# Split fp32r products for a trunk's dense projections, and a turned gather in the expert passes

## The reference

```python
z = x @ w_in + b_in                      # 1024 -> u_a 512, u_b 512, z_ga 1024, z_gb 1024
out_a = pool_mixer(u_a, ...)             # windowed means of 2, 4, 8, 16 rows, then w_pool per group
y, h  = ssm_mixer(u_b, ...)              # S5: diagonal complex recurrence, 32 groups x 64 states
out_b = gelu(y) * sigmoid(gelu(y) @ w_glu + b_glu)
merged = sigmoid(z_ga) * (out_a @ w_proj_a) + sigmoid(z_gb) * (out_b @ w_proj_b)
x = layer_norm(ALPHA * x + merged @ w_out)
# layer 0: dense SwiGLU 1024 -> 2816 -> 1024; layer 1: top 2 of 8 experts, 1024 -> 3584 -> 1024
x = layer_norm(ALPHA * x + ffn(x))
```

## Time and profile before

| | |
|---|---|
| median of 3 runs | 1784.83 us (1780.98 to 1785.2) |
| profiled execution, its own time | 1787.87 us |
| its span | 1786.0 us |
| mean granted TensorE clock | 0.976 of full |
| TensorE busy | 1730.0 us, 97% |
| VectorE busy | 1175.3 us, 66% |
| ScalarE busy | 847.6 us, 47% |
| GpSimd busy | 52.9 us, 3% |
| HBM read | 437.06 MB, 246 GB/s over the span |

### The profile page before, as it was taken

The page is one execution under the profiler, slowest core; times in us unless marked ns, Lnnn a source line. Parts: engine busy times, 40 slices in busy tenths (PEclk is TensorE's granted clock), DMA queues, the critical chain, the costliest instruction groups (busy, mean ns, idle before and its releaser), DMA issues.

```text
span 1786.0 us, 23421 instructions
## 1 busy us (share of the span) xinstructions
PE 1730.0 (97%) x8795; PEld 1422.0 (80%) x8795; DVE 1175.3 (66%) x1264; ACT 847.6 (47%) x732; POOL 52.9 (3%) x89
## 2 busy tenths in 40 slices
PE   7998999999999999999999999999999999999994
PEld 3886888888868778788888888888888888888883
DVE  6824324521130323798898888887988988988985
ACT  1221020000021111677677677776777776777771
POOL 2010000002000000200000000000000000000001
PEclk9998999999999899899999999999999999999997
DMA  8243344446422324499899899899998998998980
GB/s 252 101 134 83 126 127 143 155 150 152 159 89 85 117 76 141 153 366 371 301 372 374 300 363 375 300 377 345 317 372 322 350 377 310 361 363 304 369 336 24
DMA packets 228468, 441.67 MB, mean 247 GB/s; under 512 B 21712, under 2 KB 65664, under 8 KB 228398
## 3 DMA queue, kind: packets, MB, share of 16 engines
q1 hardware_dynamic: 210688, 432.06, 68.4%
q0 software_dynamic: 2432, 5.34, 1.5%
q10 hardware_dynamic: 15294, 3.52, 1.0%
HBM read 437.06 MB, written 1.93 MB: 246 GB/s over the span
## 4 chain that ended last, share of the span: by engine, by line
PE 89%; DVE 6%; issue 3%; ACT 1%; DMA 0%; DVEq 0%; ACTq 0%; POOL 0%
PE bank L1387 86%; PE bank L1397 3%; DVE w_lo L831 2%; DVE ssm L831 2%; DVE r_all L831 1%; ACT y_hi L770 1%; DMA wide<-in_x_sample_dram 0%; DVE ssm L1200 0%; DVE y_lo L1290 0%; DVE wide L1060 0%; DVE ssm L1350 0%; DVE scr L831 0%; DVE wide L831 0%; DVE ssm L1360 0%; DVEq L1200 0%
## 5 line engine op out<-in xcount | busy, mean ns | idle before, releaser
L831 DVE TENSOR_TENSOR w_lo<-weights,w_hi 128x2048 fp32r<-128x2048 f32 x336 | 764.9, 2289 | 123.2 <-ACT w_hi L779 119.2
L779 ACT ACTIVATE w_hi<-weights 128x2048 fp32r<-128x2048 f32 x336 | 644.3, 1920 | 209.1 <-PE bank L1387 209.0
L1387 PE MATMUL bank<-w_hi,xg_hi 128*128 128x512 f32 x896 | 357.2, 399 | 2.4 <-DVE xg_lo L831 0.7
L1387 PE MATMUL bank<-w_hi,xg_lo 128*128 128x512 f32 x896 | 350.6, 391 | 0.0
L1387 PE MATMUL bank<-w_lo,xg_hi 128*128 128x512 f32 x896 | 349.7, 390 | 0.0
L1387 PE MATMUL bank<-xT,weights 128*128 128x264 f32 x1344 | 305.0, 390 | 0.0
L1387 PEld LDWEIGHTS bank<-xT,weights 128*128 128x128 f32 x1344 | 258.1, 192 | 46.5 <-issue 1.7
L1387 PEld LDWEIGHTS bank<-w_hi,xg_hi 128*128 128x128 f32 x896 | 168.7, 188 | 41.7 <-DVE w_lo L831 4.8
L1387 PEld LDWEIGHTS bank<-w_hi,xg_lo 128*128 128x128 f32 x896 | 168.4, 188 | 36.8
L1387 PEld LDWEIGHTS bank<-w_lo,xg_hi 128*128 128x128 f32 x896 | 168.9, 189 | 33.0
L1387 PE MATMUL bank<-w_hi,hidT_hi 128*128 128x512 f32 x448 | 174.8, 390 | 0.0
(11 more groups left out here) (259 smaller groups left out, 1451.9 us busy)
## 6 DMA issues: line engine op xcount, KB each, us to landing
weights<-in_w_moe_gate_dram SPq DMA_DIRECT2D x112, 1024.0 KB, 7.0
weights<-in_w_moe_up_dram SPq DMA_DIRECT2D x112, 1024.0 KB, 7.0
weights<-in_w_moe_down_dram SPq DMA_DIRECT2D x112, 1024.0 KB, 6.8
weights<-in_w_in_dram SPq DMA_DIRECT2D x24, 1024.0 KB, 5.3
weights<-in_w_ffn_gate_dram SPq DMA_DIRECT2D x11, 1024.0 KB, 5.4
weights<-in_w_ffn_up_dram SPq DMA_DIRECT2D x11, 1024.0 KB, 5.3
weights<-in_w_out_dram SPq DMA_DIRECT2D x8, 1024.0 KB, 5.1
weights<-in_w_ffn_down_dram SPq DMA_DIRECT2D x8, 1024.0 KB, 5.2
```

The source lines that it names most:

```text
L779: act.activation(w_hi[s % PAIRS][:, :], ring_slot[:, :], ACT.Copy).then_inc(w_hi_ready, 1)
L831: return dve.tensor_tensor(out, a, b, op)
L1387: ins = pe.matmul(out, lhsT, rhs, start=start, stop=stop, skip_group_check=True)
```

## The change

**Split products in the trunk.** ub, ua, the gates, out and the dense FFN (gate, up, down) become three fp32r products of split operands. The pieces are of 512 KB (`PIECE` = 1024 elements a row), in four raw slots and four pairs of hi and lo (`RAWS`), laid where the six 1 MB slots are. ACT copies a piece to `piece_hi` (`weights_hi`), DVE subtracts into `piece_lo` (`weights_lo`); both do so as far as a table (`split_limits`) says, ahead of the tile that they empty next. 130 pieces are split. wpool, pa, glu and pb stay fp32 ("whole"). A raw slot is free once its lo part is made, a pair once TensorE has used it. Within a group of four tiles the pieces but the last two are used across all tiles first. The activations are split as well: `x_hi`, `x_lo` behind each layer norm, `m_hi`, `m_lo` for out, `h_hi`, `h_lo` for down. The residual first adds `x_hi` and `x_lo` back together.

**Order.** `s5_matrices` stands behind pa in both layers, followed by the chunk sums and y; layer 1's left the FFN. On DVE, `kernel_rows` and `states` stand behind the products with pa. The w1 table's six operations (`s5_inputs`) move from DVE to POOL, where they start once `bbar` is ready and `ut` emptied. `load_layer` moves from ACT's queue to SP's: behind the fourth piece, and before the first FFN piece.

**Passes.** `pick` is stationary and 512 columns of `xtok` stream: 12 matmuls instead of 48 give the rows (`picked`), ACT and DVE copy a half each to `xrow`, and 8 turns, which stand between the halves of the pass's last `down`, transpose them.

```diff
+RAWS = 4
+PIECE = 1024
...
-            for i, (key, src, k, n) in enumerate(plan):
-                if i == 2:
+            for i, (key, src, k, n, split) in enumerate(plan):
+                if i == RAWS:
                     load_columns(sp, COLUMNS[2:], cols_in)
...
+                    load_layer(sp, 0)
+                if key == ("w_ffn_gate", 0, 0):
+
+                    sp.wait_ge(rows_out, 16 * 2)
+                    sp.wait_ge(states_out, 16 * 4)
+                    load_layer(sp, 1)
+                if i >= RAWS:
+                    sp.wait_ge(w_lo_ready if plan[i - RAWS][4] else whole_used, place[i - RAWS] + 1)
...
+            def s5_inputs(l):
+
+                pool.wait_ge(bbar_ready, l + 1)
+                wait_emptied(pool, ("ut", l, 2))
...
+                pool.tensor_tensor(w1n[0], pw[0], mt[0], ALU.mult)
+                step(pool.tensor_tensor(t4, pw[1], mt[1], ALU.mult))
+                step(pool.tensor_tensor(w1n[0], w1n[0], t4, ALU.subtract))
+                pool.tensor_tensor(w1n[1], pw[0], mt[1], ALU.mult)
+                step(pool.tensor_tensor(t4, pw[1], mt[0], ALU.mult))
+                pool.tensor_tensor(w1n[1], w1n[1], t4, ALU.add).then_inc(w1n_ready, 1)
...
+            def weights_hi(limit):
+
+                nonlocal n_hi
+                for j in range(n_hi, limit):
+                    i = split_plan[j]
+                    act.wait_ge(piece_landed[i % RAWS], 16 * (i // RAWS + 1))
+                    if j >= RAWS:
+                        act.wait_ge(used, j - RAWS + 1)
+                    n = plan[i][2] * plan[i][3]
+                    act.activation(piece_hi[j % RAWS][:, 0:n], piece[i % RAWS][:, 0:n], ACT.Copy).then_inc(w_hi_ready, 1)
+                n_hi = max(n_hi, limit)
...
+            def weights_lo(limit):
+
+                nonlocal n_lo
+                for j in range(n_lo, limit):
+                    i = split_plan[j]
+                    n = plan[i][2] * plan[i][3]
+                    dve.wait_ge(w_hi_ready, j + 1)
+                    tt(piece_lo[j % RAWS][:, 0:n], piece[i % RAWS][:, 0:n], piece_hi[j % RAWS][:, 0:n], ALU.subtract)\
+                        .then_inc(w_lo_ready, 1)
+                n_lo = max(n_lo, limit)
...
-                    if f == 5:
-                        s5_tables(1)
-                    if f == 9:
-                        s5_outputs(1)
-                    if f == 14:
-                        s5_inputs(1)
-                kernel_rows(1)
+                    if c == 0:
+                        c_rows(1)
+                    if c == 1:
+                        s5_tables(1, (("fg", 8), ("fu", 8)))
+                s5_outputs(1, ("down", 0))
...
+                        if len(rhs) == 2:
+                            mm(ps[m], wt[p][0][:, kk, at], rhs[0](k), k == 0, False)
+                            mm(ps[m], wt[p][1][:, kk, at], rhs[0](k), False, False)
+                            mm(ps[m], wt[p][0][:, kk, at], rhs[1](k), False, end, through(sig) if last else sig)
...
-                for n in range(2):
-                    gather_tile(claim_in_pass(("gather", n), i), n)
+                rows_picked(i)
                 down(NFC - 1)
```

More of the change, by code:

```diff
@@ L69 @@
 SLOT = 2048
+RAWS = 4
+PIECE = 1024
+FGROUPS = [range(a, min(a + 4, NFT)) for a in range(0, NFT, 4)]
 MAGIC = 12582912.0
@@ L99, in weight_plan @@
+        for c in range(2):
+            add_rows(("out", l, c), w["w_out"][l][:, 512 * c:512 * c + 512])
         if l == 0:
-            for c in range(NFT // 2):
+            for c, fs in enumerate(FGROUPS):
                 for name in ("w_ffn_gate", "w_ffn_up"):
[L102 to L106, removed]
@@ L121, in psum_plan @@
 def psum_plan():
-    tiles = [(("x", k), "ad"[k % 2]) for k in range(KD // 2)] + [(("xs",), "a")]
+    tiles = [(("x", k), "d") for k in range(KD // 2)] + [(("xs",), "d")]
     def s5_matrices(l):
@@ L138, in psum_plan @@
         tiles += [(("h0", l, r), "a") for r in range(2)] + [(("rows", l, s), "a") for s in range(2)]
[L139 to L142, removed]
+        tiles += [(("mix", l, g), "a") for g in range(4)] + [(("pa", l, m), "d") for m in range(KD)]
+        tiles += s5_matrices(l) + [(("chunk", l, r), "d") for r in range(3)]
         tiles += [(("y", l, i), "ad"[i % 2]) for i in range(4)]
@@ L173, in __init__, with split_limits @@
         self.bank = {k: i % NBANK for i, k in enumerate(self.keys)}
+def split_limits(tiles, plan, groups):
+    at = {key: i for i, (key, _, _, _, _) in enumerate(plan)}
+    group_of = {t: pieces for names, pieces in groups.values() for t in names}
+    last_of = {names[-1]: pieces for names, pieces in groups.values()}
+    limits, done = {}, 0
+    for key in tiles.keys:
+        pieces = group_of.get(key, ())
+        sure = max([done] + [at[p] + 1 for p in pieces[:-2]])
+        limits[key] = sum(split for _, _, _, _, split in plan[:sure + RAWS])
+        done = max([sure] + [at[p] + 1 for p in last_of.get(key, ())])
+    return limits
 PASS_TILES = [(("g", 0), "a", 0)]
@@ L209, in trunk_kernel @@
     n_plan = len(plan)
-    slot_of = {key: i for i, (key, _, _, _) in enumerate(plan)}
+    groups = product_groups()
+    piece_at = {key: i for i, (key, _, _, _, _) in enumerate(plan)}
+    place = [sum(e[4] == plan[i][4] for e in plan[:i]) for i in range(n_plan)]
+    split_plan = [i for i in range(n_plan) if plan[i][4]]
+    n_split, n_whole = len(split_plan), n_plan - len(split_plan)
     tiles = Tiles(psum_plan())
+    split_limit = split_limits(tiles, plan, groups)
     per_pass = PassTiles()
@@ L1134, in layer_norm, with low @@
                 at = (C_LN1G + KD * l) if which == 0 else C_LN2G
+                bias = (C_LN1B + KD * l) if which == 0 else C_LN2B
+                def low(k):
+                    dve.wait_ge(x_next, KD * n + k + 1)
+                    dve.scalar_tensor_tensor(out=x_lo[:, k, :], in0=rT[:, k, :], scalar=colT[:, bias + k:bias + k + 1],
+                                             in1=x_hi[:, k, :], op0=ALU.add, op1=ALU.subtract).then_inc(x_lo_ready, 1)
                 for k in range(KD):
@@ L1137, in layer_norm, with merged_lo @@
                                              in1=y, op0=ALU.mult, op1=ALU.mult).then_inc(norm_ready, 1)
+                    if k > 0 and l < DEPTH - 1:
+                        low(k - 1)
+                if l < DEPTH - 1:
+                    low(KD - 1)
+            def merged_lo(l, m):
+                dve.wait_ge(m_hi_ready, KD * l + m + 1)
+                tt(m_lo[:, m, :], gates[:, 8 + m, :], m_hi[:, m, :], ALU.subtract).then_inc(m_ready, 1)
             def mixer(l):
@@ L1426, in project @@
[L1426 to L1442 removed]
+                    return done
@@ L1518, in mixer @@
                 for n in range(4):
-                    project([("gate", l, 4 * n + m) for m in range(4)], [("gate", l, n, h) for h in range(2)], xT)
+                    project(("gate", l, n), rows_of(x_hi, x_lo))
                 for r in range(2):
```

622 lines of the change are left out of this document (365 added, 257 removed).

## The result

The changed kernel takes 1803.76 us (median of 4 runs, 1799.7 to 1805.1) where before takes 1782.9 on the same chip (median of 4 runs: the three that gave 1784.83 and one more): a ratio of 1.0119, 95% interval 1.0094 to 1.0143. It is 1.2% slower; the forecast was 1766 us and a gain, with 1802 as the upper end of its range. Its profiled execution took 1799.7 us, span 1798.0.

What follows compares the result with a forecast made beforehand. TensorE, busy 97% of the span, was taken as the bound. FFN -24.5, layer 1's mixer -11.2, layer 0's +6.5, passes -13.8, clock +4 gave -39.0; with +20 for GpSimd, 1787.9 became 1769, less 3 is 1766 us (range 1718 to 1802).

Steps and rivals of the forecast that it cites:

- The price of a split product: Trunk matmuls: three fp32r records of 264 columns at 0.121 us replace two fp32 records, gaining 0.082 us per k-tile.
- Dense FFN: Gate and up -28.9 us, down -14.4, less waits of 9.4 and 6.4 and 3 at the start: -24.5.
- the +4: Clock term: two new waits in the FFN each cost about 2.0 us again, +4 us.
- Layer 1's ub and ua: Layer 1's first projections: cheaper split products there save 7.0 us.
- Passes: MoE passes: the gather with fewer matmuls plus transposes saves 1.73 us each, -13.8 us for eight.
- POOL's products: Gates of both layers: w1 products on GpSimd may hold VectorE's splits, 41 us lost or nothing; half taken, +20.
- VectorE is held for everything: Rival: in both layers' gates each GpSimd product holds the next split, 28 + 26 us lost, 1800 us; chance 0.22.
- The clock behind the new wait: Ahead of y in each layer: a fallen clock behind the 13.1 us wait costs 3 us.
- Layer 0's start: Layer 0 up to the gates' end: VectorE is the limit, TensorE's saving is not seen, gates end 1 us earlier.
- Out and layer norm: Out: 64 k-tiles save 5.2 us, less 4.7 waiting for VectorE's x_hi + x_lo and m_lo: -0.6 per layer.
- the +20: Half of the 41 us that VectorE, held by GpSimd's w1 products, might lose in the gates.

Runs made afterwards that it cites:

- run 2: The changed kernel with the six w1 products back on VectorE, a weight split let in after each, none on GpSimd: 1768.52 us, ratio 0.9927.
- run 1: The changed kernel with 54 idle matmuls on TensorE between the chunk sums and y in both layers: 1786.03 us, ratio 1.0014.
- Run 6: The changed kernel with the old order around the scan, w1 products on VectorE and layer 0's first weight splits let in earlier: 1735.07 us, ratio 0.9736.
- run 8: The changed kernel with 12 idle 128-column matmuls between the wait and y in both layers: 1791.85 us, ratio 1.0059.

## Why the prediction was wrong, by its own steps

**The price of a split product: right.** 54 records of ua in layer 0, the first and the last:

```profile
43.59 0.28 PE L1576 MATMUL bank<-x_hi,piece_hi 128*128 128x264 f32 x1
...
50.06 0.28 PE L1576 MATMUL bank<-x_lo,piece_hi 128*128 128x264 f32 x1
```

(50.06 - 43.59) / 53 = 0.122 us; taken were 0.121. The estimate of 112.5 ns, worked out from the stream rule of the Trainium skill, page "TensorE: Matmul & The Clock Gate", section "Back-to-back issue gap", is below the measured record, and the measurement decides. (The "some 25 us" that the prediction put on it count layer 0's gates too, whose gain it took as not seen; for its 816 k-tiles it is 21.)

**Dense FFN: right, and too cautious.** -33.7 measured; the forecast was -31.7, and +4 for its clock. Its waits on splits are 10.1 us in all, of which 6.1 lie beside the tables at 336 to 356 us (1.38, 3.05, 1.63) and 3.3 beside the products of 2304; I had 9.4, 6.4 and 3 for the start. The four pairs of buffers cover more than I let them. Of the two falls of the clock that the +4 stood for, one came, and cost 2.2 us (22 records that take 0.122 us at full clock, behind the 3.05 us wait):

```profile
340.56:345.40 4.84, 4.84 (x22) 0.50 0.46 120
```

**Layer 1's ub and ua: right** (-6.1 against -7.0). **Passes: right** (-13.4 against -13.8).

**POOL's products: the step that failed, by its choice.** The mechanism was named, its full price worked out (28 and 13), and then halved, "with one held row and three free ones". The three free rows were no evidence against it: they have an operand in PSUM, and the splits have two in SBUF. The rival "VectorE is held for everything" is what happened. Its place was right, its price (54) too high: the gates of each layer cost 19 us more than 128 k-tiles at -0.082 say (+8.8 and +8.5 against -10.5), 38 in all, and taking the products away gave 35 although VectorE got 27 us of work back. By stage, run 2 gives 13.8 us in layer 0, where I had 28, and 18.7 in layer 1, where I had 13. The 13 was right for what it priced, the waiting (12.5 us of it went with the products); the rest is TensorE's busy time, 57.8 us against 51.7, at the lower clock, for which I had nothing. The rival's 26 for layer 1 is twice the prediction's own 13, so that its 1800 lies near the measured 1804 is luck: it has 16 to 19 us too much here, and none of the losses below.

**The clock behind the new wait: the second step that failed.** The wait was right to 0.1 us (13.2 against 13.1). For what follows it I took 3 us, scaled from the 2.0 that 40 dense records lost behind 4.2 us. The work behind the new wait is another kind, y, and the clock had fallen ahead of the wait, in the chunk sums. It cost 10.9 in each layer (run 1: 10.9 back in each), 15.8 us more than charged in all. The rows of y before the change did not tell this, since there y always came behind 40 records of pa; but the row I scaled from was another kind of work, and the clock of before at 130.6 was there to be read.

**Layer 0's start: missed.** "VectorE is the limit from the start" was right, but I concluded that nothing is lost; the splits of ub and ua came behind the tables and ub's rows one by one, and the turns of ub began 11.0 us later. Run 6 got 7.5 of them back there. These are waits that the change adds (4.1, 1.4 and 7.4 us), and I had added up VectorE's busy time only, not the order of its queue.

**Out and layer norm:** +3.5 in layer 0 against -0.6; the 3.2 us wait was charged with 4.7, but a second wait of 2.1 us stands ahead of the layer norm, and the norm's averaging matmuls (`avg`) ran at a mean clock of 0.70 (5.36 us for 3.80). Not tried further.

Put together: the sum was -39.0 and the spans differ by +12.0, 51 us. Of these, 39.8 lie before the gates' ends (20.8 in layer 0, 19.0 in layer 1), for which the +20 had been put; 18.0 lie behind the two starts of y; the FFN and its clock give back 6.0; and -0.8 is all the rest.

## What to carry to other kernels

Moving work to an idle engine is free only if it shares nothing with the busy one. Before giving GpSimd an operation that reads SBUF, look at what VectorE has in its queue beside it: its operations with two SBUF inputs, and here one with a single input too, may each wait for the whole of GpSimd's, and short ones in a chain pay most for their size. Of a new wait on TensorE ask not only how long it is but what ran before it and what runs behind it: here records with a 128x128 stationary operand brought the clock back in 4 to 5 us, and y's paid the lower level to their end, so work of the first kind belongs between a stretch that lowers the clock and one that does not raise it. And where a split or a copy per piece shares a queue with tables and copies, count the order of that queue, not its busy share.

## What had not been expected of the hardware

The clock fell while TensorE was busy without a gap: 5.7 to 7.2 us into the chunk sums, in layer 0 of the kernel before and in both layers of the changed one. 192 records of y, 25.5 us without a gap, stayed at a granted clock of 0.50 from first to last, where the 24 idle records of run 8 brought it up in 5.0 us, and in the changed kernel 18 records of ua in 4.1 us, as two windows behind the wait at 57.8 us show:

```profile
57.78:61.90 4.12, 4.12 (x18) 0.50 0.65 210
61.90:65.00 3.10, 3.10 (x26) 0.97 0.63 228
```

Once at 1.00, the same y kept it for its 14.7 us. And VectorE operations of 0.17 us took 3.4 to 4.5 us beside GpSimd's products of 128x2048, while GpSimd's fills of the same memory, 24 us of them, left the two-operand rows at 1.29 and 2.21 us unchanged.
